# Expert weights loaded by four transfers for each 2 MB part in place of one

## What is computed

```python
def moe_ffn(hn, w_router, b_router, w_gate_up, b_gate_up, w_down, b_down):
    ...
    top_vals, top_idx = lax.top_k(logits, TOP_K)          # TOP_K = 4 of 32
    gates = jax.nn.softmax(top_vals, axis=-1)
    ...
    h = lax.ragged_dot(xs, w_gate_up, group_sizes) + b_gate_up[e_sorted]
    glu = jnp.minimum(h[:, ::2], SWIGLU_LIMIT)
    lin = jnp.clip(h[:, 1::2], -SWIGLU_LIMIT, SWIGLU_LIMIT)
    act = glu * jax.nn.sigmoid(SWIGLU_ALPHA * glu) * (lin + 1.0)
    y = lax.ragged_dot(act, w_down, group_sizes) + b_down[e_sorted]
    y = y * gates.reshape(-1)[order].astype(y.dtype)[:, None]
    out = jax.ops.segment_sum(y, tok, num_segments=T)
```

## Time and profile before

| | before |
|---|---|
| median of three runs | 2747.82 us |
| the profiled execution: its own time | 2741.76 us |
| its span (first to last instruction) | 2740.0 us |
| PE busy | 2625.3 us (96%) |
| DVE, ACT, POOL busy | 1113.7, 594.5, 587.7 us |
| packets of q1, MB, share of the 16 DMA engines | 92408, 503.72, 50.0% |
| packets of q0, MB, share | 23840, 51.56, 7.4% |
| loads of slots: count, KB each, median us to landing | 192, 2048, 8.0 (gate and up) and 7.7 (down) |

### The profile page before, as it was taken

The page is one execution under the profiler, slowest core; times in us unless marked ns, Lnnn a source line. Parts: engine busy times, 40 slices in busy tenths (PEclk is TensorE's granted clock), DMA queues, the critical chain, the costliest instruction groups (busy, mean ns, idle before and its releaser), DMA issues.

```text
span 2740.0 us, 50019 instructions
## 1 busy us (share of the span) xinstructions
PE 2625.3 (96%) x17629; PEld 2168.7 (79%) x17630; DVE 1113.7 (41%) x2667; ACT 594.5 (22%) x1348; POOL 587.7 (21%) x566
## 2 busy tenths in 40 slices
PE   9999999999999996999999999999999999999997
PEld 8777766666487774999999999998787878787875
DVE  1111155563223334533344434434444444445444
ACT  1333255553111111011111111111111112121212
POOL 0000031122001111111123212312323322323232
PEclk9999999999999998999999999999999999999998
DMA  8111243324200004856667677877888888888885
GB/s 290 52 54 54 66 140 97 89 92 157 69 1 23 31 31 165 327 205 222 226 241 267 244 282 262 283 284 285 298 319 306 317 294 312 294 314 304 318 293 213
DMA packets 116322, 556.29 MB, mean 203 GB/s; under 512 B 26435, under 2 KB 61187, under 8 KB 91672
## 3 DMA queue, kind: packets, MB, share of 16 engines
q1 hardware_dynamic: 92408, 503.72, 50.0%
q0 software_dynamic: 23840, 51.56, 7.4%
HBM read 507.16 MB, written 64.72 MB: 209 GB/s over the span
## 4 chain that ended last, share of the span: by engine, by line
PE 57%; issue 2%; DVE 1%; another core or an unknown queue 0%; DMA 0%; DVEq 0%; ACT 0%; ACTq 0%; POOLq 0%
PE bank L1461 38%; PE wide L1927 8%; PE wide L1893 8%; PE wide L1454 1%; PE wide L1934 1%; DVE h_out L2600 0%; DMA xg<-d_xn,gidx 0%; ACT y_sb L1400 0%; PE wide L2008 0%; PE bank L1851 0%; DVEq L2512 0%; DMA out_h<-h_out 0%; DVEq L2601 0%; ACTq L1401 0%
## 5 line engine op out<-in xcount | busy, mean ns | idle before, releaser
L1461 PE MATMUL bank<-xe_t,slot 128*128 128x128 f32 (+4 forms) x8192 | 1066.3, 290 | 51.1 <-issue 47.9
L1461 PEld LDWEIGHTS bank<-xe_t,slot 128*128 128x128 f32 x8192 | 1038.5, 194 | 71.5 <-issue 69.9
L2506 DVE TENSOR_SCALAR glu<-bank,b_gu 128x256 f32<-128x256 f32 x256 | 123.9, 484 | 784.1 <-PE bank L1461 635.2
L1406 ACT ACTIVATE sig<-glu 128x256 f32<-128x256 f32 x256 | 106.7, 417 | 930.1 <-DVE glu L2506 821.5
L1042 POOL DMA_INDIRECT xg_q<-d_xq,gidx x256 | 263.7, 1030 | 194.9 <-issue 108.7
L1068 POOL DMA_INDIRECT d_sum<-y_sb,sidx x62 | 103.1, 1662 | 831.0 <-ACTq L1387 776.6
L1927 PE MATMUL wide<-slot,act_t 128*128 128x512 f32 x570 | 248.3, 593 | 0.3 <-issue 0.3
L1893 PE MATMUL wide<-act_t,slot 128*128 128x144 f32 (+3 forms) x1664 | 233.6, 302 | 0.4 <-DVE act_t L2518 0.4
L1893 PEld LDWEIGHTS wide<-act_t,slot 128*128 128x128 f32 x1664 | 231.9, 190 | 0.7 <-DVE act_t L2518 0.7
L1927 PEld LDWEIGHTS wide<-slot,act_t 128*128 128x128 f32 x570 | 107.1, 191 | 128.0 <-issue 127.1
L1423 ACT ACTIVATE y_t<-wide 128x256 f32<-128x256 f32 x248 | 81.6, 381 | 371.8 <-PE wide L1893 189.6
(11 more groups left out here) (314 smaller groups left out, 2522.5 us busy)
## 6 DMA issues: line engine op xcount, KB each, us to landing
slot<-in_w_gu SPq DMA_DIRECT2D x128, 2048.0 KB, 8.0
slot<-in_w_dn SPq DMA_DIRECT2D x64, 2048.0 KB, 7.7
w_in<-in_w_in SPq DMA_DIRECT2D x1, 6144.0 KB, 24.7
w_mem_k<-in_w_mem_kv SPq DMA_DIRECT2D x4, 1024.0 KB, 10.9
w_mem_v<-in_w_mem_kv SPq DMA_DIRECT2D x1, 4096.0 KB, 21.2
x_sb<-in_x SPq DMA_DIRECT2D x8, 512.0 KB, 3.4
cneg<-d_cneg SPq DMA_DIRECT2D x8, 512.0 KB, 6.8
d_vw<-mix_out SPq DMA_DIRECT2D x16, 256.0 KB, 2.2
```

Of the source, the lines that this page charges most:

```text
L1406: ac.activation(sig[m % 2][:, :], glu[m % 2][:, :], ACT.Sigmoid, scale=1.702).then_inc(e_sig, 1)
L1461: m = pe.matmul(dst, l, r_, start=(k == 0), stop=(k == n - 1))
L2506: ve.tensor_scalar(glu[b][:, :], pp[b][:, 0:CAP], b_gu[:, bass.ds(e * 2 * KD + 2 * m, 1)], 7.0, ALU.add, ALU.min).then_inc(e_glu, 1)
```

## The change

Each load of a slot is cut along k into four transfers of two slices, [128, 2, 512], 512 KB each. A partition's run in one transfer is 2 x 512 x 4 = 4096 bytes. All four raise the slot's `full` by 16, so the waits ask for 64 * (i + 1). No buffer, no order between slots and no other instruction changes.

```diff
+        W_PIECES = 4
...
+            def load_part(c, e):
+                for k in range(0, KD, KD // W_PIECES):
+                    now = slice(k, k + KD // W_PIECES)
+                    load(slots[c][:, now, :], expert_part(c, e)[:, now, :], e_w[c].full)
...
-            load(slots[0][:, :, :], expert_part(0, first), e_w[0].full)
+            load_part(0, first)
...
-            load(slots[1][:, :, :], expert_part(1, first), e_w[1].full)
+            load_part(1, first)
...
             for c in range(2, SLOTS):
-                load(slots[c][:, :, :], expert_part(c, first), e_w[c].full)
+                load_part(c, first)
...
                 for c in range(SLOTS):
                     sp.wait_ge(e_w[c].free, i)
-                    load(slots[c][:, :, :], expert_part(c, e), e_w[c].full)
+                    load_part(c, e)
...
-                        pe.wait_ge(e_w[c].full, 16 * (i + 1))
+                        pe.wait_ge(e_w[c].full, 16 * W_PIECES * (i + 1))
```

More of the change, by code:

```diff
@@ L1899, in e_down_first @@
             def e_down_first(i, w):
-                pe.wait_ge(e_w[4].full, 16 * (i + 1))
+                pe.wait_ge(e_w[4].full, 16 * W_PIECES * (i + 1))
                 for m in (0, 2):
@@ L1911, in e_down @@
                     if m == 4:
-                        pe.wait_ge(e_w[5].full, 16 * (i + 1))
+                        pe.wait_ge(e_w[5].full, 16 * W_PIECES * (i + 1))
                     if m >= 4 and m % 2 == 0:
@@ L1919, in e_rows_down @@
                 for hd in range(2):
-                    pe.wait_ge(e_w[4 + hd].full, 16 * (i + 1))
+                    pe.wait_ge(e_w[4 + hd].full, 16 * W_PIECES * (i + 1))
                     rows_free(hd, i, 1)
```

## The result

Four runs of the changed kernel took 2782.69 to 2794.96 us, median 2792.88; four of the kernel before 2739.43 to 2748.08, median 2746.48. The ratio is 1.0167, its 95% interval 1.0136 to 1.0197: slower by 46 us where 2747 was forecast, and outside the range that ended at 2772. The profiled execution is the shortest of the four, 2782.69 us with a span of 2780.9; its span is 40.9 us above that of before.

The account below looks back on a forecast made before the run. PE was taken as the bound, busy 2625.3 of 2740.0 us, with weights early. Terms 0 + 0 + 0 - 0.5 + 0 = -0.5 us gave a 2747.3 us median; range 2741 to 2753, 8 in 10 2700 to 2772.

Parts of the forecast that it names:

- Step 1: SP's queue: 576 extra issues take 248 to 703 us, fitting in its 1273.7 us of waiting; cost 0.
- Step 2: PE's waits ask for 64 in place of 16, same instructions at the same places; cost 0.
- Step 3: Weight loads: pieces overlap at 3% less rate, DMA busy 0.85 to 0.93 of a width-128 item; cost 0.
- Step 4: First item, PE's wait for its gather: slightly shorter, -0.5 us, bounds -3.5 to +0.2 us.
- Step 5: Later items' gathers beside smaller pieces: PE's holes taken as unchanged, 0 us, between -50 and +25 at width 128.
- C: PE's holes at the gathers grow as short packets and rows flow together: 2766 us half, 2785 full; chance 0.24.
- B: PE's holes at the gathers shrink without long packets: 2719 us if halved, 2687 if gone; chance 0.36.
- D: Weight loads: pieces do not overlap and loads become the bound, over 300 us more at width 128; chance 0.02.
- nothing on the path: Whole kernel, the likeliest case: PE waits for no slot, so the time stays at 2747 us; chance 0.38.

Follow-up runs that it names:

- the same first run: Kernel before with weights laid out in rows of 4096 bytes, still one transfer a slot: 2738.71 us, ratio 0.9976.

## Why the prediction was wrong

*Step 1, more issues on SP: right.* SP's two waits are together 932.7 us against 1273.7, 341 us less or 0.59 us an issue, inside the 0.43 to 1.22 that were taken, and slots 0 and 3 to 5 in pieces cost nothing that can be measured (1.0009).

*Step 2, the waits for 64: right.* No wait of PE for a slot.

*Step 3, the bytes in pieces: right.* The DMA engines are busy for 0.87 and 0.92 of the two items shown, where 0.85 to 0.93 was said, and rows of 4096 bytes in one transfer gave 0.9976. The packets came to 175,352, above the 166,000 named, by the 16 for each extra transfer.

*Step 4, the first item: right to its size.* PE waits 7.1 us for `xg`, before 7.23: -0.1 us, where -0.5 was taken of bounds -3.5 to +0.2.

*Step 5, the gathers meet the pieces: this is the step that failed.* Its term was put at 0 between -50 and +25 us at width 128, and it measured +30.7 us there and +10.1 us in the wider items. Why it failed the runs show: the 192 extra transfers of slots 1 and 2, which go out about the gathers, cost 39.1 us by themselves and the other 384 cost 1.0 us. The value 0 was taken from item 16 as the nearest row, on the ground that a load overlaps the gathers there too. That row holds one transfer beside them at a time, and what the change multiplies is transfers. The upper end failed as well: it was set by the worst item of before, 47.34 us, as if a hole could not grow beyond the longest one seen. Item steps of about 48 us are now the rule.

*Two readings were off, without harm to the sum.* SP's queue is idle for 1273.7 of about 1670 us of the experts' stage, three quarters and not half. And the holes of item 16 are not of one size: they take 0.27 to 0.47 us.

*The rivals.* C named the right place and sign at 0.24, with 2766 us at half and 2785 at full price; 2793 came. Its reason, short packets and gathers' rows flowing together, is refuted by rows of 4096 bytes in one transfer (PE's "issue" 46.8 us, about as before); the tiny transfers cost 1.0096 with the weights in long packets. So C had the place right and its reason wrong. B, the holes shrink since no long packet stands in the way, is refuted in its size by the same first run: at most its 6.7 us are there, of the 28 or 60 that B named. D did not come. The Trainium skill's rule against small transfers (DMA: Bandwidth & Descriptors, Rules for kernel authors) would have given the sign, but not by what it says: the rule is on bandwidth, and nobody waited for a load on the chips that lost, while the same 512 KB loads cost nothing where the ratio is 1.0001.

*What the forecast missed above all.* The prediction took the holes for a property of the kernel. They depend on where the kernel runs as well. From 2745.45 to 2669.18 us the kernel before differs by 76 us between chips; the chain of before against the changed kernel on the chip without holes gives 52.6 us at width 128 (779.69 - 727.07) and 17.4 us before it (1881.98 - 1864.61), 70 in all. The forecast of "nothing on the path" holds to 0.1% there. Each chip was used once, so that the chip cannot be told from something else that changed between sessions. Why some sessions show the holes is open; so is what in PE's supply is held up while POOL and SP both issue. The traces show only that no semaphore and no slot is awaited, that the holes come with the gathers, that they move with them into the wider items' down product, that transfers issued among them lengthen them, and that transfers of 4 KB suffice for about two thirds of the loss. No profile of the kernel before was taken on the chips without holes; that it has none there is read from the kernels beside it and its time.

## What to carry to other kernels

Where POOL issues indirect transfers in a stretch of small matmuls, do not price the transfers that another queue adds in that stretch at nothing because their bytes are small or early (here 192 of them cost 39 us, 384 elsewhere about 1, and 192 of 4 KB still 25). Treat holes that wait for no semaphore as a cost that can grow past the worst one seen, and try to move their trigger beside wide matmuls: beside those of 512 columns they went away, beside those of 144 to 208 they did not. Before such holes are explained or repaired, run the unchanged kernel on another chip: where the holes did not exist, the loss of 1.67% was zero, and late gathers, which had gained 0.54%, cost 0.1 to 0.6% in the forms run there.

## What the runs showed of the hardware

- One and the same kernel took 2745.45, 2725.85, 2726.83, 2669.61 and 2669.18 us on five chips, each figure a median of its one session. The granted clock in the profiled execution of the changed kernel was 0.978 on the chip with long holes and 0.989 on the one with none.
- Three 4 KB transfers behind each of two loads of 2 MB cost 25.4 us in 32 items, with PE waiting for none of them.
- Loads of 512 KB to 32 partitions landed after 16.6 us (gate and up, median), and those of 512 KB to 128 partitions after 6.0 us in the changed kernel (median from 1200 to 2740 us), though four of either are issued in a row.
- Gathers moved beside the down product left PE no hole at width 128, where it consists of matmuls 512 columns wide, and 12.6 to 14.3 us of them where it consists of matmuls 144 to 208 columns wide.
